# Mixture-of-experts rounds: token tiles held in TensorE and 512 weight columns moved past them, experts ranked by count, rounds of 192, 192, 128, 192, 128 and then 256 slots

## The chip, the cores and the metric

The kernel runs on one core of one Trainium2 chip. The metric is the device time of the program in microseconds (us). All matmuls of the part studied here are fp32-precision products put together from rounded halves, as described below.

## The reference

One inference step of a two-layer backbone on 640 tokens (128 of a prompt, 512 of a sample), width 1024. Each layer is a token mixer followed by a feed-forward part; in layer 0 that is a dense SwiGLU, in layer 1 it is a choice of 2 of 8 SwiGLU experts of inner width 1408. Only the last is touched by the change:

```python
logits = (hf @ router).astype(jnp.float32)
top_v, top_i = lax.top_k(logits, TOP_K)                       # TOP_K = 2, N_EXP = 8
wts = jax.nn.softmax(top_v, axis=-1)
gate = jnp.sum(jax.nn.one_hot(top_i, N_EXP, dtype=jnp.float32) * wts[..., None], axis=-2)
g, u = jnp.split(jnp.einsum('nd,edf->nef', hf, w_gu), 2, axis=-1)     # w_gu: 8 x 1024 x 2816
act = jax.nn.silu(g) * u * gate[..., None].astype(h.dtype)
return jnp.einsum('nef,efd->nd', act, w_down).reshape(B, T, D)        # w_down: 8 x 1408 x 1024
```

The 640 tokens make 1280 choices. Worked out from the reference and its inputs, experts 0 to 7 are chosen 177, 226, 132, 229, 147, 106, 48 and 215 times.

## The kernel before

The function `moe` runs `experts` (routing, then the expert rounds) and `combine` (gather of the two results of each token, residual, final norm). In `experts` the engines have one program each, tied together by semaphores.

Routing: the tokens are normed, the router product gives the logits, VectorE (DVE) works out each choice's slot (L2474 to L2482) and a table of rounds, ScalarE (ACT) copies the transposed tokens into `htok` (semaphore `h_tok`), and GpSimd (POOL) scatters them to `slots_h` in HBM by ten indirect DMAs (L2553). Slots are handed out in blocks of `BLK` = 256, as many blocks per expert as it needs, in the order of the experts.

Rounds: a hardware loop (`Fori`) does one block of 256 slots at a time. A round of the inputs used here belongs to one expert. In a round:

- SyncE (SP) loads the next block of slots and the expert's weights, 11 blocks j of 128 inner columns, each as two 512 KB gate-up transfers (L2246) and one 512 KB down transfer (L2248), into a ring `raw` of three slots.
- ACT rounds each piece to fp32r (`w_hi`, L2409) and DVE computes the rest (`w_lo` = raw - `w_hi`, L2514), so that a product is made of three: hi x hi, hi x lo, lo x hi.
- TensorE (PE) transposes the block of slots (L2335). For each j the gate-up product (L2360) holds 128x128 of weights as the stationary operand and moves 256 slots; its result lies with the inner columns on partitions, so it can be the stationary operand of the down product (L2347) as it is, which moves 512 weight columns. PE works on gate-up of j, then on down of j-1.
- ACT takes the silu of the gate half (L2421), DVE multiplies by the up half (L2524), and the two split the product into `act_hi` (L2425) and `act_lo` (L2526).
- At the end ACT and DVE split the next block (L2399, L2506), split the first weights of the next round, and copy the finished 256x1024 block out; POOL stores it (L2562).

## Time and profile before

| | |
|---|---|
| time, median of 3 runs | 2706.48 us (2704.94 to 2707.95) |
| profiled execution, first to last instruction | 2713.9 us |
| granted TensorE clock, mean over the span | 0.947 of full speed |
| PE busy | 2386.3 us, 88% |
| weight loads (PEld) busy | 2177.9 us, 80% |
| DVE busy | 1444.5 us, 53% |
| ACT busy | 1069.2 us, 39% |

No time of its own is given for the profiled execution beside its span, which is 7.4 us above the median of the runs. A busy engine in this table need not set the time; which one does is read stage by stage. The expert rounds run from 1893.42 us to about 2657.3 us of the span.

### The profile page before, as it was taken

What the parts mean: (1) busy time and instruction counts of PE and PEld (TensorE: products, weight loads), DVE (VectorE), ACT (ScalarE), POOL (GpSimd) and SP (SyncE); (2) the same over time, 40 slices, a digit from 0 to 9 for tenths busy, and PEclk for the clock granted to TensorE, in tenths of its full rate; (3) what the DMA queues carried; (4) which work ended last, traced back from release to release, by engine and by line L of the source; (5) the groups of instructions that cost most, each with busy time, mean ns of one, the idle gap of its engine ahead of it and who ended that gap; (6) DMA issues with size and microseconds to landing.
All of it is one profiled execution on the core that took longest, in us unless ns stands there. A gap on an engine that the chain in (4) does not pass through costs nothing. (4 is left out here: it accounts for less than half of the span.)

```text
span 2713.9 us, 47159 instructions
## 1 busy us (share of the span) xinstructions
PE 2386.3 (88%) x19349; PEld 2177.9 (80%) x19349; DVE 1444.5 (53%) x2038; ACT 1069.2 (39%) x1753; POOL 335.3 (12%) x347
## 2 busy tenths in 40 slices
PE   5996687888899999989967788895999999999993
PEld 4985465778899999989845667794999999999992
DVE  5577556774422222245665667743555555555556
ACT  4332136673422112143321366633444444444443
POOL 0055333001000000000553330012000000000002
PEclk8998899999899999989988999997999999999996
DMA  5332764703122322222127200025676676567664
GB/s 209 94 85 45 203 209 160 248 1 94 47 78 59 90 78 63 59 57 87 56 53 205 90 6 1 1 63 194 181 231 204 181 230 207 173 196 238 196 183 163
DMA packets 453116, 340.49 MB, mean 125 GB/s; under 512 B 90961, under 2 KB 421151, under 8 KB 451935
## 3 DMA queue, kind: packets, MB, share of 16 engines
q1 hardware_dynamic: 436383, 277.43, 35.2%
q10 hardware_dynamic: 11520, 41.95, 4.8%
...
## 5 line engine op out<-in xcount | busy, mean ns | idle before, releaser
L2360 PE MATMUL ps<-h_hi,w_hi 128*128 128x256 f32 x1408 | 399.5, 284 | 1.6 <-DVE h_lo L2506 1.6
L2360 PE MATMUL ps<-h_hi,w_lo 128*128 128x256 f32 x1408 | 399.0, 283 | 0.0
L2360 PE MATMUL ps<-h_lo,w_hi 128*128 128x256 f32 x1408 | 399.0, 283 | 0.0
L2514 DVE TENSOR_TENSOR w_lo<-w_raw,w_hi 128x2048 fp32r<-128x2048 f32 (+1 forms) x180 | 309.1, 1756 | 119.0 <-ACT w_hi L2409 119.0
L2360 PEld LDWEIGHTS ps<-h_hi,w_hi 128*128 128x128 f32 x1408 | 270.6, 192 | 4.7 <-issue 2.0
L2360 PEld LDWEIGHTS ps<-h_lo,w_hi 128*128 128x128 f32 x1408 | 270.7, 192 | 2.8
L2360 PEld LDWEIGHTS ps<-h_hi,w_lo 128*128 128x128 f32 x1408 | 270.6, 192 | 0.0
L2409 ACT CAST w_hi<-w_raw 128x2048 fp32r<-128x2048 f32 (+1 forms) x180 | 256.4, 1474 | 0.1
L2747 PE MATMUL ps<-ffn_h_hi,w_hi_ffn 128*128 128x320 f32 x704 | 161.9, 311 | 5.5 <-DVE ffn_h_lo L378 4.2
L2421 ACT ACTIVATE tokens_then_blocks<-ps 128x256 f32<-128x256 f32 x88 | 33.8, 384 | 325.8 <-PE ps L2360 325.7
L2747 PE MATMUL ps<-ffn_h_lo,w_hi_ffn 128*128 128x320 f32 x704 | 161.3, 311 | 0.0
L2747 PE MATMUL ps<-ffn_h_hi,w_lo_ffn 128*128 128x320 f32 x704 | 161.3, 311 | 0.0
L1849 DVE TENSOR_TENSOR p_lo<-ps,p_hi 128x512 fp32r<-128x512 f32 (+1 forms) x196 | 123.4, 631 | 50.9 <-ACT p_hi L1921 46.9
L2524 DVE TENSOR_TENSOR tokens_then_blocks<-tokens_then_blocks,ps 128x256 f32<-128x256 f32 x88 | 37.0, 421 | 199.0 <-ACT tokens_then_blocks L2421 199.0
L1921 ACT CAST p_hi<-ps 128x512 fp32r<-128x512 f32 (+1 forms) x196 | 106.3, 542 | 87.4 <-PE ps L1738 87.3
L1844 DVE TENSOR_REDUCE tm<-ps 128x1 f32<-128x768 f32 (+1 forms) x140 | 114.8, 821 | 43.6 <-PE ps L1714 29.0
L1738 PE MATMUL ps<-cst,tm 128*128 128x128 f32 x700 | 115.5, 284 | 23.1 <-DVE p_lo L1849 23.0
L571 PE MATMUL ps<-w_hi_in,h_hi 128*128 128x454 f32 x320 | 122.4, 382 | 4.6 <-DVE w_lo_in L152 3.1
L2747 PEld LDWEIGHTS ps<-ffn_h_hi,w_hi_ffn 128*128 128x128 f32 x704 | 118.3, 189 | 6.7 <-issue 6.7
L571 PE MATMUL ps<-w_lo_in,h_hi 128*128 128x454 f32 x320 | 119.2, 373 | 0.0
L2747 PEld LDWEIGHTS ps<-ffn_h_lo,w_hi_ffn 128*128 128x128 f32 x704 | 118.5, 189 | 0.0
L571 PE MATMUL ps<-w_hi_in,h_lo 128*128 128x454 f32 x320 | 118.5, 370 | 0.0
...
## 6 DMA issues: line engine op xcount, KB each, us to landing
...
```

What stands on the lines that cost most here:

```text
L571: mm = pe.matmul(ps[:, t, 0:TMT], x[:, 4 * half + k, t * P:(t + 1) * P], wt[:, tile % 2, k * TMT:(k + 1) * TMT], start=(half == 0 and k == ...
L1738: mm = pe.transpose(ring(j)[:, q * P:(q + 1) * P], prob_block(u, t, k) if t else prob_slot(u, 0), self.ident)
L1844: dve.tensor_reduce(low[:, u % 2, t:t + 1], score_tile(u, t), AX.X, ALU.min).then_inc(s["least"], 1)
L1849: dve.tensor_tensor(place(p_lo, j), turned(j), place(p_hi, j).bitcast(F32), ALU.subtract).then_inc(s["lo"], 1)
L1921: act.copy(place(p_hi, j), turned(j)).then_inc(s["hi"], 1)
L2360: mm = pe.matmul(ps[:, j % 2, half * BLK:(half + 1) * BLK], gu(wt, j, half, k), x[:, k, :], start=(k == 0 and n == 0), stop=(k == KC - 1 a ...
L2409: act.copy(whi[:, q, part], raw[:, q, part]).then_inc(s["hi_d" if down else "hi_u"], 1)
L2421: act.activation(sg[:, j % 2, :], ps[:, j % 2, 0:BLK], ACT.Silu).then_inc(s["silu"], 1)
L2514: dve.tensor_tensor(wlo[:, q, part], raw[:, q, part], whi[:, q, part].bitcast(F32), ALU.subtract).then_inc(s["lo_d" if down else "lo_u"], 1)
L2524: dve.tensor_tensor(g, g, ps[:, j % 2, BLK:2 * BLK], ALU.mult).then_inc(s["prod"], 1)
L2747: mm = pe.matmul(ps[:, 4 * (j % 2) + 2 * half + st, 0:b - a], wt[:, u, o:o + P], x[:, k, a:b], start=(k == 0 and m == 0), stop=(k == KC - ...
```

## The change

Experts are ranked by their number of choices, expert 0 put first in any case. The first five rounds are written out, with a fixed number of slots each (`SIZES`); the ranks that they serve are in `REGION`: 0, 3, 1, 4, 2. The three experts with the most choices get the 256-slot rounds of a loop, and what does not fit an expert's round goes to further rounds of 256. With the counts above that is the order 192 (177 choices), 192 (132), 128 (48), 192 (147), 128 (106), 256 (215), 256 (226), 256 (229), with no further round.

In a round the slots are tiles of 128 that are held as the stationary operand, and 512 weight columns (256 of gate, 256 of up) move: the 11 column blocks become `NU` = 6 units u, the last of half width, in 17 pieces of 1 MB (`ORDER`), which land in a ring of six slots (`RAW`) and are split into a ring of five (`HL`). The product now lies with the slots on partitions, so PE turns it (`turn_act`) before the down product, and ACT and DVE make `act_hi` and `act_lo` from the turned one. In a 192-slot round the tile of the last 64 slots ("few") is multiplied in plain fp32, from `raw`, without split: two matmuls of 64 stationary columns each, one writing partitions 0 to 63 and one 64 to 127.

Cut to its core:

```diff
-RMAX = 2 * T // BLK + NE - 1
+STATIC = 5
+RMAX = NE + 5
...
-        SL = 3
...
+        NU, PW, SMALL = 6, 2048, 64
+        ORDER = [("g", 0, 0), ("g", 0, 1), ("g", 1, 0), ("g", 1, 1), ("d", 0, 0)]
+        for u in range(2, NU):
+            ORDER += [("g", u, a) for a in range(2 if u < NU - 1 else 1)] + [("d", u - 1, 0)]
+        ORDER += [("d", NU - 1, 0)]
+        NP = len(ORDER)
+        RAW, HL = 6, 5
...
+            hT = raw[:, 2 * PW:2 * PW + KC * T].rearrange("p (c t) -> p c t", c=KC)
...
+            SIZES = (192, 192, 128, 192, 128)
+            REGION = (0, 3, 1, 4, 2)
...
+            def tiles_of(c):
+                return {128: (0,), 192: (1, 0), 256: (0, 1)}[c]
...
+            def groups(c):
+                return {128: ((0, 0, 3), (0, 1, 0)), 192: ((0, 0, 3), (1, None, 0), (0, 1, 1)),
+                        256: ((0, 0, 3), (0, 1, 0), (1, 0, 1), (1, 1, 3))}[c]
...
+            def wait_raw_free(eng, r, n):
+                if is_first(r) and n < 0:
+                    return
+                eng.wait_ge(s["w_hi"], count("pieces", r, n + 1))
+                eng.wait_ge(s["w_lo"], count("pieces", r, n + 1))
+                if isinstance(r, int) and size(r - 1 if n < 0 else r) == 192:
+                    kind, u, _ = ORDER[n % NP]
+                    if kind == "g":
+                        eng.wait_ge(s["gu"], tile_count(r - 1 if n < 0 else r, u, 1))
+                    else:
...
-                    for j in range(SL):
-                        load_w(0, j)
+                    for n in range(2):
+                        load_w(0, n)
+                    sp.wait_ge(s["h_tok"], 2 * NT)
+                    for n in range(2, RAW):
+                        load_w(0, n)
...
+                    def feed(r):
+                        sp.wait_ge(s["h_turned"], count("groups", r, 0, 1))
+                        load_block(next_size(r), region_of(r + 1) if isinstance(r, int) else r + (STATIC + 1))
...
+                    def multiply(r, u, tile):
+                        c = size(r)
+                        bank = gate_bank(c, u, tile)
+                        last = tile == tiles_of(c)[-1]
+                        if u == 0:
+                            pe.wait_ge(s["h_lo"], count("groups", r, 0, 1) if last else count("groups", r, 2))
+                        elif c > 128:
+                            pe.wait_ge(s["prod"], tile_count(r, u - 1, tile))
+                        elif u >= 2:
+                            pe.wait_ge(s["prod"], tile_count(r, u - 2, tile))
+                        if few(c, tile):
+                            half = columns(u) // 2
+                            for k in range(KC):
+                                n = at("g", u, k // 4 if u < NU - 1 else 0)
+                                if k in (0, 4):
+                                    pe.wait_ge(s[f"raw{raw_slot[n]}"], count_raw(raw_slot[n], r, landed[n]))
+                                w_ = gate_up_raw(u, k)
+                                for q in range(2):
+                                    mm = pe.matmul(ps[64 * q:64 * q + 64, bank, 0:2 * half].rearrange("p (h n) -> p h n", h=2),
+                                                   h_few[:, k], w_[:, :, q * half:(q + 1) * half], start=(k == 0), stop=(k == KC - 1))
+                            mm.then_inc(s["gu"], 1)
+                            return
+                        for k in range(KC):
+                            if k == 0 or k == 4 and u < NU - 1:
+                                pe.wait_ge(s["w_lo"], count("pieces", r, at("g", u, k // 4) + 1))
+                            for n, (x, wt) in enumerate(((hhi, whi), (hhi, wlo), (hlo, whi))):
+                                mm = pe.matmul(ps[:, bank, 0:2 * columns(u)], x[:, k, tile * P:(tile + 1) * P], gate_up(wt, u, k),
+                                               start=(k == 0 and n == 0), stop=(k == KC - 1 and n == 2))
...
+                        if few(c, tile) and u < NU - 1:
+                            mm = pe.transpose(ps[:, 2, 256:256 + P], act_tok[:, 1, 0:P], self.ident)
...
+                    def down(r, u, tile):
+                        c = size(r)
+                        pe.wait_ge(s["a_lo"], unit_done(r, u))
+                        pe.wait_ge(s["w_lo"], count("pieces", r, at("d", u) + 1))
+                        if u == 0 and not is_first(r):
+                            pe.wait_ge(s["y_act"], count("rounds", r))
+                            pe.wait_ge(s["y_dve"], count("rounds", r))
+                        for b in range(blocks_of(u)):
+                            st, sp_ = u == 0 and b == 0, u == NU - 1 and b == blocks_of(u) - 1
+                            if few(c, tile):
+                                for half in range(2):
+                                    mm = pe.matmul(ps[64 * half:64 * half + 64, 6, :], a_few[:, u % 2, b], down_rows_raw(u, b, half),
+                                                   start=st, stop=sp_)
...
+                    def work(r):
+                        c = size(r)
+                        order = tiles_of(c)
+                        coming = groups(next_size(r))
+                        for u in range(NU):
+                            for tile in order:
+                                multiply(r, u, tile)
+                            for tile in order[:-1]:
+                                turn_act(r, u, tile)
+                            if u:
+                                down(r, u - 1, 0)
+                                if c == 256:
+                                    down(r, u - 1, 1)
+                            turn_act(r, u, order[-1])
+                            if u == NU - 3:
+                                pe.wait_ge(s["blk_in"], count("blocks", r, PER["blocks"][next_size(r)], 1))
+                                turn_group(coming[0])
+                            if u == NU - 1:
+                                for n, g in enumerate(coming[1:]):
+                                    if n == 2:
+                                        pe.wait_ge(s["h_lo"], count("groups", r, 1, 1))
+                                    turn_group(g)
+                            if u and c == 192:
+                                down(r, u - 1, 1)
+                        for tile in range(len(order)):
+                            down(r, NU - 1, tile)
+                    for r in range(STATIC):
+                        work(r)
                     with pe.Fori(0, rounds) as r:
-                        pe.wait_ge(s["h_lo"], 4 * r + 4)
-                        for j in range(FC):
...
+                    def split(r, n, ahead=0):
+                        q = raw_slot[n]
+                        act.wait_ge(s[f"raw{q}"], count_raw(q, r, per_round[q] * ahead + landed[n]))
+                        wait_used(act, r, hl_before[n] + NP * ahead)
+                        act.copy(part(whi, n), raw_piece(n)).then_inc(s["w_hi"], 1)
...
+                    def work(r):
+                        c = size(r)
+                        order = tiles_of(c)
+                        coming = len(groups(next_size(r)))
+                        for u in range(NU - 1):
+                            gate(r, u, order[0])
+                            split(r, 3 * u + 2)
+                            for tile in order[1:]:
+                                gate(r, u, tile)
+                            take(r, u, order[0])
+                            split(r, 3 * u + 3)
+                            for tile in order[1:]:
+                                take(r, u, tile)
+                            split(r, 3 * u + 4)
+                        for tile in order:
+                            gate(r, NU - 1, tile)
+                        upper(r, next_size(r), 0, 1)
+                        for tile in order:
+                            take(r, NU - 1, tile)
+                        for m in range(1, coming):
+                            upper(r, next_size(r), m, 1)
+                        for n in range(2):
+                            split(r, n, 1)
+                        act.wait_ge(s["dn"], count("units", r, NU))
+                        if not is_first(r):
+                            act.wait_ge(s["y_free"], count("rounds", r))
+                        last = act.copy(y[:, 0, 0:512], ps[:, 4, :])
+                        if c == 192:
+                            last = act.copy(y[:, 0, 512:D], ps[:, 5, :])
+                        elif c == 256:
+                            last = act.copy(y[:, 1, 0:512], ps[:, 6, :])
+                        last.then_inc(s["y_act"], 1)
+                    for r in range(STATIC):
+                        work(r)
...
+                    chain(dve.scalar_tensor_tensor(out=key[:], in0=counts, scalar=16.0, in1=key0[:], op0=ALU.mult, op1=ALU.add))
+                    chain(dve.tensor_tensor(tri[:], bcast_mid(key[:], NE), bcast_last(key[:], NE), ALU.is_lt))
+                    chain(dve.tensor_reduce(region[:], tri[:], AX.X, ALU.add))
+                    chain(dve.tensor_scalar(wide[:], region[:], -1.5, None, ALU.add), wait=False)
+                    chain(dve.tensor_scalar(high[:], region[:], STATIC - 0.5, float(SMALL), ALU.is_ge, ALU.mult), wait=False)
+                    chain(dve.tensor_scalar(home[:], region[:], float(BLK), None, ALU.mult))
+                    chain(dve.tensor_tensor(wide[:], wide[:], wide[:], ALU.mult))
+                    chain(dve.tensor_scalar(wide[:], wide[:], 1.0, float(SMALL), ALU.is_ge, ALU.mult))
```

Of the routing, DVE's chain from the counts to the slots has 23 instructions where it had 8. The functions `gate`, `take`, `lower` and `split` of DVE stand in the same order as those of ACT in `work`.

Three places of the order of instructions. First PE, at the last column block of a 256-slot round before; `tokens_then_blocks` is the block of slots to be turned.

```order
L2360 MATMUL ps<-h_hi,w_hi 128x256
L2360 MATMUL ps<-h_lo,w_hi 128x256
L2360 MATMUL ps<-h_hi,w_lo 128x256
L2332 ISA
L2335 MATMUL ps<-cst,tokens_then_blocks 128x128 x4
L2347 MATMUL ps<-w_hi,act_hi 128x512 x2
L2347 MATMUL ps<-w_lo,act_hi 128x512 x2
L2347 MATMUL ps<-w_hi,act_lo 128x512 x2
```

The same engine with the change, in a unit of a 128-slot round; here `tokens_then_blocks` is the product to be turned.

```order
L2539 MATMUL ps<-w_lo,h_hi 128x512
L2539 MATMUL ps<-w_hi,h_lo 128x512
L2576 MATMUL ps<-w_hi,act_hi 128x512 x2
L2576 MATMUL ps<-w_lo,act_hi 128x512 x2
L2576 MATMUL ps<-w_hi,act_lo 128x512 x2
L2576 MATMUL ps<-w_hi,act_hi 128x512 x2
L2576 MATMUL ps<-w_lo,act_hi 128x512 x2
L2576 MATMUL ps<-w_hi,act_lo 128x512 x2
L2556 MATMUL ps<-cst,tokens_then_blocks 128x128 x2
L2539 MATMUL ps<-w_hi,h_hi 128x512
```

The gate-up product now moves 512 columns, and two transposes stand between the down product of unit u-1 and the gate-up product of unit u+1.

Second PE with the change in a 192-slot round, from the turn of the few tile to the next unit.

```order
L2549 MATMUL ps<-cst,tokens_then_blocks 128x128
L2576 MATMUL ps<-w_hi,act_hi 128x512 x2
L2576 MATMUL ps<-w_lo,act_hi 128x512 x2
L2576 MATMUL ps<-w_hi,act_lo 128x512 x2
L2556 MATMUL ps<-cst,tokens_then_blocks 128x128 x2
L2571 MATMUL ps<-w_raw,act_few 64x512 x4
L2531 MATMUL ps<-w_raw,tokens_then_blocks 64x256 x16
L2539 MATMUL ps<-w_hi,h_hi 128x512
```

The matmuls of 64 stationary columns stand beside those of 128, with a change between the two shapes four times in a unit.

Third DVE, before, in two column blocks of a round.

```order
L2524 TENSOR_TENSOR tokens_then_blocks<-tokens_then_blocks,ps 128x256
L2526 TENSOR_TENSOR act_lo<-tokens_then_blocks,act_hi 128x256
L2513 REGISTER_ALU
L2514 TENSOR_TENSOR w_lo<-w_raw,w_hi 128x2048
L2514 TENSOR_TENSOR w_lo<-w_raw,w_hi 128x1024
L2522 REGISTER_ALU
L2524 TENSOR_TENSOR tokens_then_blocks<-tokens_then_blocks,ps 128x256
```

And DVE with the change, in a unit of a 128-slot round and the start of the next; L2805 is the product with the up half, L2817 makes `act_lo`.

```order
L2805 TENSOR_TENSOR tokens_then_blocks<-tokens_then_blocks,ps 128x256
L2799 TENSOR_TENSOR w_lo<-w_raw,w_hi 128x2048
L2817 TENSOR_TENSOR act_lo<-ps,act_hi 128x2x128
L2799 TENSOR_TENSOR w_lo<-w_raw,w_hi 128x2048 x2
L2805 TENSOR_TENSOR tokens_then_blocks<-tokens_then_blocks,ps 128x256
```

A piece of weights now stands between the product and `act_lo`, and the second piece that the next unit needs stands behind `act_lo`, which waits for PE's transposes.

## Rows read from the trace of the kernel before

**Rows 1.** The head of the profile page.

```profile
span 2713.9 us, 47159 instructions
```

**Rows 2.** Busy time by stage, one round: us, busy of each engine, PEclk, DMA share, GB/s.

```profile
2083.00:2178.00 95.00, 95.00 (x677) 89.50 (x676) 50.61 (x50) 43.13 (x51) 0.75 (x1) 1.00 0.67 204
```

**Rows 3.** PE in order of time, last column blocks of a round: start us, us.

```profile
2079.01 0.60 PE L2335 MATMUL ps<-cst,tokens_then_blocks 128*128 128x128 f32 x4
2079.36 0.71 PE L2347 MATMUL ps<-w_hi,act_hi 128*128 128x512 f32 x2
2079.91 0.62 PE L2347 MATMUL ps<-w_lo,act_hi 128*128 128x512 f32 x2
2080.37 0.63 PE L2347 MATMUL ps<-w_hi,act_lo 128*128 128x512 f32 x2
...
2085.52 0.28 PE L2360 MATMUL ps<-h_lo,w_hi 128*128 128x256 f32 x1
2085.64 0.28 PE L2360 MATMUL ps<-h_hi,w_lo 128*128 128x256 f32 x1
```

**Rows 4.** PE in order of time, first and last matmuls of the rounds.

```profile
1893.42 0.57 PE L2360 MATMUL ps<-h_hi,w_hi 128*128 128x256 f32 x1 [1.59 <-DVE h_lo L2506]
...
2656.71 0.61 PE L2347 MATMUL ps<-w_hi,act_lo 128*128 128x512 f32 x2
```

**Rows 5.** Groups by line and shape, the round of rows 2: busy us, mean ns, idle before.

```profile
L2514 DVE TENSOR_TENSOR w_lo<-w_raw,w_hi 128x2048 fp32r<-128x2048 f32 x11 | 25.2, 2294 | 14.4 <-ACT w_hi L2409 14.4
L2409 ACT CAST w_hi<-w_raw 128x2048 fp32r<-128x2048 f32 x11 | 20.9, 1904 | 0.0
...
L2506 DVE TENSOR_TENSOR h_lo<-ps,h_hi 128x512 fp32r<-128x512 f32 x4 | 2.6, 685 | 0.6 <-ACT h_hi L2399 0.6
```

**Rows 6.** ACT and DVE in order of time, one column block.

```profile
2188.01 0.38 ACT L2421 ACTIVATE tokens_then_blocks<-ps 128x256 f32<-128x256 f32 x1
2188.88 0.41 ACT L2425 CAST act_hi<-tokens_then_blocks 128x256 fp32r<-128x256 f32 x1 [0.49 <-DVE tokens_then_blocks L2524]
2189.19 2.85 ACT L2409 CAST w_hi<-w_raw 128x2048 fp32r<-128x2048 f32 x2
...
2188.43 0.42 DVE L2524 TENSOR_TENSOR tokens_then_blocks<-tokens_then_blocks,ps 128x256 f32<-128x256 f32 x1 [2.30 <-ACT tokens_then_blocks L2421]
2191.12 3.43 DVE L2514 TENSOR_TENSOR w_lo<-w_raw,w_hi 128x2048 fp32r<-128x2048 f32 x2 [1.38 <-ACT w_hi L2409]
```

**Rows 7.** PE in the mixer: matmuls of 64 and 32 stationary columns, and the clock.

```profile
340.46 1.61 PE L1012 MATMUL ps<-conv_in_out 128*64 128x128 f32 x24
342.00 0.64 PE L1077 MATMUL ps<-G_decay,oA 128*32 128x256 f32 x8
342.57 0.27 PE L1143 MATMUL ps<-X_turned,Y 64*64 64x64 f32 x1
...
279.96 1.08 PE L1077 MATMUL ps<-G_decay,oA 128*32 128x256 f32 x8
280.82 1.08 PE L1077 MATMUL ps<-oA 128*32 128x256 f32 x8
...
340.50:343.00 2.50, 2.50 (x48) 1.82 (x48) 1.67 (x3) 0.90 (x2) 0.74 (x1) 1.00 0.84 323
279.96:281.80 1.84, 1.84 (x18) 0.59 (x16) 0.00 (x0) 0.48 (x1) 1.00 (x1) 0.50 0.67 111
```

**Rows 8.** Busy time by stage, a stretch of full DMA queues, columns as in rows 2.

```profile
2085.00:2099.00 14.00, 14.00 (x109) 13.55 (x108) 9.27 (x9) 8.31 (x10) 0.75 (x1) 1.00 1.08 355
```

**Rows 9.** The scatter of the tokens by stage, then DVE's chain ahead of it.

```profile
1863.00:1884.00 21.00, 1.55 (x8) 1.15 (x6) 8.43 (x13) 8.31 (x9) 13.73 (x10) 0.56 0.64 252
...
1861.51 0.22 DVE L2477 TENSOR_REDUCE first_slot<-by_expert 128x8 f32<-128x64 f32 x1
1861.76 0.20 DVE L2478 TENSOR_TENSOR place<-ps,first_slot 128x40 f32<-128x40 f32 x1
```

**Rows 10.** Busy time by stage, a stretch of the mixer with an interrupted PE.

```profile
1720.00:1760.00 40.00, 32.70 (x241) 30.74 (x240) 28.66 (x51) 26.49 (x61) 0.00 (x0) 0.91 0.01 1
```

536 lines of the change are left out of this document (338 added, 198 removed).

## The prediction

> **What bounds the kernel now.** I read the page's head first (span 2713.9 us [rows 1]), then busy time by stage. In a middle round PE is busy 95.00 of 95.00 us at the full clock, DVE 50.6, ACT 43.1, and the DMA engines 0.67 of the time at 204 GB/s [rows 2]: PE alone sets the length of a round. Next PE in order of time, for what an instruction really takes, since a busy time counts a matmul until its result is out. Starts lie 0.12 us apart for 256 moving columns, a pair of 512-column matmuls takes 0.46 us (0.229 each), four transposes 0.35 us (0.088 each) [rows 3]. A round has 528 gate-up matmuls, 132 down matmuls and 16 transposes: 528 x 0.12 + 132 x 0.229 + 16 x 0.088 = 63.4 + 30.2 + 1.4 = 95.0 us, which is the row. Eight rounds run from 1893.4 to 2657.3 us [rows 4], 763.9 us with a slow first microsecond or two. Eight is also what the counts give (none is over 256). So the rounds are 28% of the span, and of their 2048 slots 1280 hold a choice.
>
> **The change, part by part.**
>
> *Slots.* With the counts given, the rounds are 192, 192, 128, 192, 128, 256, 256, 256, no spill.
>
> *Full tiles.* A tile of 128 slots takes 120 gate-up matmuls of 512 columns and 24 of 256 (last unit): 120 x 0.229 + 24 x 0.12 = 30.4 us, and 66 down matmuls, 15.1 us [rows 3]. Turning the product is new: 11 transposes, 1.0 us. With 8 transposes for the block, 0.7 us, PE has 47 us of work in a 128-slot round and 94.1 in a 256-slot round, 0.9 less than now. The wider move pays 3.0 us there, since the 13 ns over the array's own time are paid once for 512 columns, not for 256; the turning takes 1.9 of them back.
>
> The Trainium skill ("TensorE: Matmul & The Clock Gate", Back-to-back issue gap) puts the gap at N/2.4 + 2.5 ns. By it wider moves would be worth 0.8 us, not 3.0, and a 256-slot round would come out 1 us longer than before. The rows show 13 to 16 ns, so I go by them.
>
> *The few tile.* Plain fp32 with 32 stationary columns in four groups: 8 records of 256 columns take 0.86 us at a granted clock of 0.50, the 1.2 GHz level, so four matmuls side by side, two records each, four clocks a column. With 64 stationary columns, two groups, 24 records of 128 columns take 1.54 us at the full clock, 0.064 each against 0.053 for the array alone: 11 ns more [rows 7]. So a few record costs 0.118 us at 256 columns and 0.224 at 512. Gate-up: 160 x 0.118 + 32 x 0.064 = 20.9 us; down: 44 x 0.224 = 9.9; in all 30.8 us where a full tile would take 45.5. The bounds: 28.2 at no overhead, and 34 at 20% over the array's time as in the 24 records. Changing the shape 24 times a round: the 8 records at full clock take 0.57 us, 0.06 more than their own time with a change ahead and behind [rows 7]; 0.05 each, 1.2 us. So 192 slots take 47 + 0.7 + 30.8 + 1.2 = 80 us.
>
> The skill ("TensorEngine Tiling (Array Packing)", Key Properties) says that a change of the tiling mode drains TensorE. A drain is some 0.16 us (a matmul's 0.28 us busy less its 0.12 us spacing [rows 3]), so by that rule it would be 4 us a round, 8 us more over three rounds. The 0.57 us speak against it.
>
> *Who waits in a 128-slot round.* Here PE's 8.4 us a unit come near what ACT and DVE need for three pieces, and the order of the instructions decides. From the end of a gate-up product: silu 0.15 us later, the ACT split of the next piece 0.31 after its start, the DVE split 1.93 after that start (2188.43, 2189.19, 2191.12) [rows 6], taking 2.29 us [rows 5]: first piece ready at 4.7 us, while PE has finished its down product (2.75) and turned (3.0). ACT and DVE make `act_hi` and `act_lo` before the second piece: `act_lo` until 5.1; `w_lo` of the second piece from 5.4 to 7.65. PE's first half of the gate-up product, 2.75 us, ends at 7.5, its second half starts at 7.75, and its result is there at 10.6. The unit takes 10.6 us, not 8.4. A round: 5.5 for the first product, four units of 10.6, 7.8 for the half-width one, 5.0 for the rest: 60.7 us, and 47 if I am wrong about the order. Weights are no bound: 18.3 MB in 60.7 us are 302 GB/s, against 355 with 512-byte to 4 KB packets mixed [rows 8], and loads have a lead of two units.
>
> *Between rounds* DVE splits the new block (0.69 us a group [rows 5]), then two pieces, 2.3 us each, before the first gate-up product can start. By the same steps the stall of PE is 2.2 us from 192 to 128 (the first piece's place is freed late, by the few tile's down product), 4.1 from 128 to 256, 2.6 from 256 to 256, none into a 192-slot round, whose few tile needs no split and covers the 2.3 us.
>
> *Routing.* DVE's chain has 15 instructions more ahead of the scatter, 0.25 us each [rows 9], some without a wait: 3.3 us. Four pieces (4.2 MB) are now loaded from the time that the tokens are turned, on the same DMA engines as the scatter, which moves 252 GB/s for 21 us [rows 9] of the 355 possible [rows 8]. The spare 2.2 MB in that time cover half, the rest is some 5 us of delay; a smaller first block gives 0.7 back. Taken: 7 us (3 if the loads slip in between, 12 if none does). Afterwards DVE copies the last block out behind a wider piece: 0.7 us.
>
> *The sum.* 3 x 80 + 2 x (60.7 + 2.2) + (94.1 x 3 + 4.1 + 2 x 2.6) + 1.5 for the slow first microseconds = 240 + 125.8 + 291.6 + 1.5 = 659 us for 763.9: 105 less. With 7.7 for routing and end it is 97 less. Against its own span that is 2713.9 - 97 = 2617; the runs' median lies 7.4 below the span, and I carry the difference over: 2706.5 - 97 = 2609 us.
>
> **The rivals.**
>
> *The order costs nothing* (PE keeps its pace because pieces are ready earlier than I follow): 27 us less in the 128-slot rounds, 9 to 14 at the round edges: 2570 us. For it: DVE has only 45 us of work in such a round. Against: both are in-order queues, and the second piece stands behind `act_lo`. 0.17.
>
> *More waits than I count*: the few tile at 34 us with a drain at each change (10 + 8 us), DMA hiccups in the 128-slot rounds, where each unit asks for 3.1 MB and a late piece stops ACT, DVE and PE in turn (10 to 20 us each). Or the clock: PE is busy 8.4 of 10.6 us a unit in a 128-slot round. In the mixer 32.7 of 40 us gave 0.91 [rows 10], which would add 5 us a round; if it stayed at the 1.2 GHz level, a unit would be 16.8 us and the two rounds 66 us longer. I put this case at 2665 us, 2632 to 2700. 0.26.
>
> *The few tile does not run side by side*, slower than before. With array time and drain one after the other, a 256-column record takes 0.213 + 0.16 us, a 512-column one 0.427 + 0.16: 160 x 0.373 + 32 x 0.267 + 44 x 0.587 = 94 us for 30.8, 190 us over three rounds: 2799 us. It takes half of that, 97 us, to lose the whole gain. Against it stand both rows at 0.057 to 0.064 us a record [rows 7]; for it that those products were short, and that here weights stream from `raw` while DMA writes there. 0.04.
>
> *The change doesn't do what it says*: other counts would bring spill rounds of 94 us each, and one takes all of the gain. Before, a count over 256 would have made a ninth round; there were eight, but 128 and 192 are not tested by that. 0.02, within 0.2% or slower.
>
> **How the numbers follow.** The forecast (2609 us, its own range 2585 to 2632) has 0.51. The two cases beside it hold 0.43; the range takes in the first down to 2568 and the lower half of the second: 2568 to 2655 leaves about 0.2 out. 0.2% is 5.4 us, about what a measurement of this kernel tells from no change. Faster: 0.94; same 0.01; slower 0.05.
>
> **What would show it.** In the profile after: PE starts 0.229 us apart at the gate-up line, 512 columns; records of 64 stationary columns 0.118 us apart; a 192-slot round of 80 us and a 256-slot round of 97 (94.1 if the edges cost nothing). In a 128-slot round PE waits twice a unit for `w_lo`, some 1.7 and 0.3 us, and the gate-up products end 10.6 us apart; 8.4 would be the first rival. The first gate-up product comes some 7 us later than 1893.4. I would be wrong if a wait for `raw` or the block's transfer stood in the 128-slot rounds, if PEclk fell there, or if the few tile took 40 us or more.

## The result and the profile after

The changed kernel takes 2635.4 us (median of 4 runs, 2629.4 to 2642.2), the kernel before 2707.2 us in the same comparison: a ratio of 0.9717, 95% interval 0.9689 to 0.9744. It is 72 us faster; 97 were forecast, 2609 us. The number lies inside the range, 26 us above the forecast and just outside the likeliest case's own range.

The head of the profile page after, which answers to [rows 1]: the span, PE's busy time and the granted clock in 40 slices.

```profile
span 2633.4 us, 42344 instructions
...
PE 2267.8 (86%) x17219; PEld 1955.9 (74%) x17219; DVE 1417.6 (54%) x1995; ACT 1029.8 (39%) x1666; POOL 334.8 (13%) x353
...
PEclk8999798999899999998997998989799999999996
```

The span is 80.5 us shorter. Busy time by stage comes next, cut at the first gate-up matmul of each of the eight rounds and at the end of the last down product (columns as in [rows 2], which they answer to).

```profile
1895.31:1978.37 83.06, 81.95 (x483) 57.30 (x485) 43.22 (x44) 36.08 (x37) 0.00 (x0) 0.98 0.57 183
1978.37:2061.19 82.82, 79.84 (x476) 55.98 (x473) 48.55 (x45) 39.58 (x40) 1.70 (x3) 1.00 0.70 235
2061.19:2126.78 65.59, 54.90 (x237) 43.12 (x237) 41.89 (x32) 33.33 (x33) 1.66 (x3) 0.92 0.88 295
2126.78:2209.63 82.85, 79.86 (x475) 56.03 (x475) 48.79 (x46) 40.09 (x40) 0.56 (x1) 1.00 0.66 218
2209.63:2277.24 67.61, 53.41 (x238) 42.31 (x238) 44.77 (x35) 37.68 (x37) 1.64 (x3) 0.95 0.90 311
2277.24:2377.94 100.70, 97.04 (x459) 80.30 (x459) 49.87 (x47) 40.15 (x46) 0.56 (x1) 0.98 0.62 202
2377.94:2477.05 99.11, 95.46 (x458) 79.11 (x458) 50.47 (x48) 40.91 (x48) 0.73 (x1) 1.00 0.60 196
2477.05:2573.98 96.93, 95.44 (x458) 79.12 (x458) 48.30 (x47) 38.79 (x46) 0.71 (x1) 1.00 0.58 189
```

The expert stage takes 678.7 us, where it took 763.9 [rows 4]; 659 had been forecast. So the direction and most of the size are in the rounds, as worked out, and 20 us of the miss are too. Where PE was busy without a break before [rows 2], it is not any more: 11 to 14 us of each 128-slot round are idle, and the granted clock is below 1.00 in them and in two others.

PE in order of time at the start of the first 128-slot round shows both (start us, us, and in brackets the idle time before and what ended it).

```profile
2061.19 0.47 PE L2539 MATMUL ps<-w_hi,h_hi 128*128 128x512 f32 x1 [1.88 <-DVE w_lo L2799]
2061.50 0.40 PE L2539 MATMUL ps<-w_lo,h_hi 128*128 128x512 f32 x1
...
2063.03 0.63 PE L2539 MATMUL ps<-w_hi,h_hi 128*128 128x512 f32 x1
2063.45 0.63 PE L2539 MATMUL ps<-w_lo,h_hi 128*128 128x512 f32 x1
...
2069.46 0.44 PE L2556 MATMUL ps<-cst,tokens_then_blocks 128*128 128x128 f32 x2 [0.93 <-DVE tokens_then_blocks L2805]
2073.12 0.80 PE L2539 MATMUL ps<-w_hi,h_hi 128*128 128x512 f32 x1 [3.22 <-DVE w_lo L2799]
...
2075.42 0.63 PE L2539 MATMUL ps<-w_hi,h_lo 128*128 128x512 f32 x1
2075.84 0.63 PE L2539 MATMUL ps<-w_hi,h_hi 128*128 128x512 f32 x1
...
2086.43 0.47 PE L2539 MATMUL ps<-w_hi,h_hi 128*128 128x512 f32 x1 [1.74 <-DVE w_lo L2799]
2086.73 0.40 PE L2539 MATMUL ps<-w_lo,h_hi 128*128 128x512 f32 x1
2086.96 0.40 PE L2539 MATMUL ps<-w_hi,h_lo 128*128 128x512 f32 x1
```

Four idle stretches in 26 us. After the one of 1.88 us and the one of 3.22 us matmuls of 512 columns start 0.42 us apart, not 0.229: TensorE is at the 1.2 GHz level. The second unit's gate-up product lasts from 2073.12 to 2081.73, 8.6 us for 24 matmuls, where the same product in a later unit takes 5.84 to 5.95.

DVE in order of time in the second and third unit of that round, to be read against the steps forecast from [rows 6]:

```profile
2082.19 0.42 DVE L2805 TENSOR_TENSOR tokens_then_blocks<-tokens_then_blocks,ps 128x256 f32<-128x256 f32 x1 [4.39 <-ACT tokens_then_blocks L2645]
2083.99 2.29 DVE L2799 TENSOR_TENSOR w_lo<-w_raw,w_hi 128x2048 fp32r<-128x2048 f32 x1 [1.37 <-ACT w_hi L2639]
2086.20 0.42 DVE L2817 TENSOR_TENSOR act_lo<-ps,act_hi 128x256 fp32r<-128x256 f32 x1
2086.93 4.49 DVE L2799 TENSOR_TENSOR w_lo<-w_raw,w_hi 128x2048 fp32r<-128x2048 f32 x2 [0.31 <-ACT w_hi L2639]
2092.76 0.42 DVE L2805 TENSOR_TENSOR tokens_then_blocks<-tokens_then_blocks,ps 128x256 f32<-128x256 f32 x1 [1.34 <-ACT tokens_then_blocks L2645]
```

Gate to gate is 10.57 us, as forecast. DVE stands idle for 3.0 us of it (1.37, 0.31 and 1.34), each time for ACT, and the piece that PE wants is done only at 2086.28, just ahead of PE's start at 2086.43. Ahead of the rounds, PE's last wait for the scatter and the first gate-up product:

```profile
1886.84 4.61 PE L2499 MATMUL ps<-w_hi 128*128 128x512 f32 x10 [25.14 <-DMA slots_h<-tokens_then_blocks,slot_of_choice]
...
1895.31 1.12 PE L2531 MATMUL ps<-w_raw,tokens_then_blocks 128*64 128x256 f32 x4 [0.78 <-DVE tokens_then_blocks L2791]
```

The routing stage's first matmul starts at 1836.43 (1839.48 in the kernel before), so from there to the first gate-up product it is 58.9 us for 53.9 before. To the first issue of the scatter it is 26.0 us for 23.6, from there until PE is released 24.4 for 19.9, and from that to the first product 8.5 for 10.5.

### The profile page after: what moved, and what is told of

It is laid out like the page before. It is cut to its first block and busy times, and to the rows that moved or that the text cites. A ratio compares the mean times of both kernels' runs of the same rounds, so it can differ in the third digit from the quotient of the medians.

```text
span 2633.4 us, 42344 instructions
## 1 busy us (share of the span) xinstructions
PE 2267.8 (86%) x17219; PEld 1955.9 (74%) x17219; DVE 1417.6 (54%) x1995; ACT 1029.8 (39%) x1666; POOL 334.8 (13%) x353
## 5 line engine op out<-in xcount | busy, mean ns | idle before, releaser
L2539 PE MATMUL ps<-w_hi,h_hi 128*128 128x512 f32 (+1 forms) x528 | 205.9, 390 | 32.2 <-DVE w_lo L2799 32.2
L2539 PE MATMUL ps<-w_lo,h_hi 128*128 128x512 f32 (+1 forms) x528 | 200.1, 379 | 0.0
L2539 PE MATMUL ps<-w_hi,h_lo 128*128 128x512 f32 (+1 forms) x528 | 199.8, 378 | 0.0
L2539 PEld LDWEIGHTS ps<-w_hi,h_hi 128*128 128x128 f32 x528 | 101.5, 192 | 63.3 <-issue 26.5
L2645 ACT ACTIVATE tokens_then_blocks<-ps 128x256 f32<-128x256 f32 (+2 forms) x84 | 29.0, 346 | 277.5 <-PE ps L2539 232.9
L3079 PEld LDWEIGHTS ps<-ffn_h_hi,w_lo_ffn 128*128 128x128 f32 x704 | 118.6, 189 | 0.0
L2143 DVE SCALAR_TENSOR_TENSOR xT<-ps,mod,xT 128x128 f32<-128x128 f32 (+2 forms) x96 | 36.3, 433 | 152.9 <-PE ps L3090 102.7
L1912 ACT ACTIVATE tm<-ps,tm 128x768 f32<-128x768 f32 (+1 forms) x140 | 111.7, 798 | 14.7 <-DVE tm L1845 14.6
## 6 DMA issues: line engine op xcount, KB each, us to landing
slots_h<-tm SPq DMA_DIRECT2D x14, 1024.0 KB, 11.2
```

The costliest lines, as they stand in the source:

```text
L1912: act.activation(prob_slot(u, t), x.rearrange("p (a n) -> p a n", a=3) if t else x, ACT.Exp, scale=-1.0, bias=low[:, u % 2, t:t + 1], accu ...
L2143: dve.scalar_tensor_tensor(out=x, in0=self.ps[:, 2 * (m % 4) + half, a - a0:b - a0], scalar=self.mod[:, l, gate, m, j:j + 1], in1=x, op0=A ...
L2539: mm = pe.matmul(ps[:, bank, 0:2 * columns(u)], x[:, k, tile * P:(tile + 1) * P], gate_up(wt, u, k), start=(k == 0 and n == 0), stop=(k == ...
L2645: act.activation(act_tok[:, tile, 0:wd], ps[:, gate_bank(c, u, tile), 0:wd], ACT.Silu).then_inc(s["silu"], 1)
L3079: mm = pe.matmul(ps[:, 4 * (j % 2) + 2 * half + st, 0:b - a], wt[:, u, o:o + P], x[:, k, a:b], start=(k == 0 and m == 0), stop=(k == KC - ...
```

## The experiments

All round lengths below are taken as above, from the first gate-up matmul of a round to that of the next; "stage" is from the first of them to the end of the last down product. A ratio is to the kernel before on the same chip. Microseconds:

```
kernel       rounds 1 to 7                                      stage
changed      83.06 82.82 65.59 82.85 67.61 100.70 99.11         678.7
again        83.08 82.83 65.56 82.83 67.64 100.67 99.09         678.7
all256       99.38 100.73 99.12 99.13 100.63 100.59 99.09       797.2
nofew        99.15 99.73 67.50 99.72 67.52 100.64 99.15         732.0
oneside      111.44 110.34 64.36 110.38 67.71 100.42 100.78     762.4
first128     83.13 82.83 62.99 82.83 66.61 100.72 99.14         675.2
both128      81.60 82.86 51.37 82.85 55.56 100.69 99.11         651.0
fill128      83.08 82.83 62.73 82.82 64.73 101.81 99.14         674.1
both_late    80.25 81.46 51.85 81.49 55.82 101.02 102.62        654.9
loadslate    82.60 82.83 65.32 82.85 67.49 100.64 99.13         679.4
edge         83.35 82.82 64.08 82.85 66.71 98.20 98.57          673.9
combo        80.23 81.47 51.89 81.49 54.92 99.77 98.55          645.7
combo_fill   81.08 81.47 51.62 81.48 54.67 98.14 98.58          644.2
```

**all256**: every round 256 slots wide.

```
-            SIZES = (192, 192, 128, 192, 128)
+            SIZES = (256, 256, 256, 256, 256)
...
-                    for g in groups(size(0)):
+                    for n, g in enumerate(groups(size(0))):
+                        if n == 3:
+                            pe.wait_ge(s["h_lo"], 1)
                         turn_group(g)
...
-                    chain(dve.tensor_tensor(wide[:], wide[:], high[:], ALU.add))
+                    chain(dve.tensor_scalar(wide[:], wide[:], 0.0, float(P), ALU.mult, ALU.add))
```

The wait is for the fourth group of the first block, and the last pair gives every expert a wide slot region.

> All eight expert rounds are made 256 slots wide; tokens stay the stationary operand and 512 weight columns move, the order of the work is the changed kernel's. So this is the first part of the change alone (and the routing chain, less what sorts experts by size). Theory (the gain comes from the round sizes, the new orientation by itself costs a little): a 256-round of the changed kernel took 99.1 us from start to start and the last one 97, so the expert stage is 7 x 99.1 + 97 = 791 us against 678.7 in the changed kernel, and the time 2635 + 112 = 2747 us, about 1.5% slower than the kernel before, whose eight rounds took 763.9 us. Rival (the orientation itself brings a part of the gain, as fewer and longer matmuls): a round is no longer than the 95.5 us of the kernel before, stage 764 us or less, time 2720 us or less.

Ratio 1.0140 (1.0111 to 1.0169): the new orientation, with its order of work, loads and routing chain but without the sizes, makes the kernel 1.4% slower; all of the gain comes from the sizes. The stage is 6 us longer than expected, which is the clock: four drops of 1.6 us. Busy time by stage, the first 11 us of the second, third and fourth round (the column after the five engines' busy times is the granted clock):

```profile
2001.30:2012.30 11.00, 11.00 (x41) 8.92 (x42) 5.12 (x5) 2.90 (x4) 0.77 (x1) 0.84 0.81 284
2102.03:2113.03 11.00, 11.00 (x49) 9.07 (x50) 6.21 (x5) 3.18 (x5) 0.75 (x1) 1.00 0.81 284
2201.15:2212.15 11.00, 11.00 (x49) 9.06 (x50) 5.99 (x5) 2.91 (x4) 0.70 (x1) 1.00 0.82 278
```

All three follow the same 2.24 us of waiting for `w_lo`; in one the clock fell to 0.84 over these 11 us and the round was 1.6 us longer. That happened in four of the seven rounds behind such an edge.

**nofew**: the 192-slot rounds become 256-slot ones.

```
-            SIZES = (192, 192, 128, 192, 128)
+            SIZES = (256, 256, 128, 256, 128)
...
-                    chain(dve.tensor_scalar(wide[:], wide[:], 1.0, float(SMALL), ALU.is_ge, ALU.mult))
-                    chain(dve.tensor_tensor(wide[:], wide[:], high[:], ALU.add))
+                    chain(dve.tensor_scalar(wide[:], wide[:], 1.0, float(P), ALU.is_ge, ALU.mult))
```

The wait of all256 for the first block's fourth group is in it too; the last lines fit the slot regions to the sizes.

> The three rounds of 192 slots become rounds of 256: the 64-token tile with fp32 matmuls in two column groups goes, its place is taken by a second full tile in three split passes. Two rounds of 128 stay. Theory (the two column groups run side by side, a 192-round is worth 82.9 us against 99.1): three rounds x 16.2 us = 48.6 us longer, 2684 us. Rival (the small tile saves less, since its shape changes and its first unit's 1.11 us wait for its turned activations go with it): 256-rounds in these places take 96 us, three x 13 = 39 us, 2674 us. If the small tile brought nothing, 2635 us.

Ratio 0.9906 (0.9876 to 0.9935), 2691 us on a chip where the kernel before took 2716.6: 53 us more than the changed kernel by the stage, 48.6 expected. The few tile is worth 16 to 17 us a round; the rest of the difference is 1.9 us in one 128-slot round and a clock drop of 1.6 us in the last round.

**oneside**: the pairs of the few tile on the same 64 partitions.

```
-  mm = pe.matmul(ps[64 * q:64 * q + 64, bank, 0:2 * half] ...
+  mm = pe.matmul(ps[0:64, bank, 0:2 * half] ...
-  mm = pe.matmul(ps[64 * half:64 * half + 64, 6, :], a_few ...
+  mm = pe.matmul(ps[0:64, 6, :], a_few ...
```

The flags that start and end a sum go with it (not shown).

> The two matmuls of each pair of the few tile (64 stationary tokens) write the same 64 partitions instead of partitions 0 to 63 and 64 to 127, so they cannot lie side by side; same count, same columns, same data. The outputs of the 64-token tiles are not those of the reference. Theory (the pair runs side by side in the changed kernel: 0.11 us a record of 256 columns, where one alone would need twice that): 0.21 to 0.24 us a record, the unit's few gate-up 7 us instead of 3.6 and few down 3.8 instead of 1.9, some 5.3 us a unit, 32 us a round, 95 us for the three: 2730 us, and the gain over the kernel before is gone. Rival (the matmuls are back to back anyway and the pairing brings nothing): 2635 us.

2723.6 us in its one run, the kernel before 2714.3 (median). The groups by line and shape over the two first rounds (busy us, mean ns) have the same 320 and 88 records; first the changed kernel:

```profile
L2531 PE MATMUL ps<-w_raw,tokens_then_blocks 128*64 128x256 f32 x320 | 37.9, 391 | 0.8 <-DVE tokens_then_blocks L2791 0.8
...
L2571 PE MATMUL ps<-w_raw,act_few 128*64 128x512 f32 x88 | 21.5, 606 | 0.0
```

and then oneside:

```profile
L2531 PE MATMUL ps<-w_raw,tokens_then_blocks 128*64 128x256 f32 x320 | 72.3, 385 | 0.8 <-DVE tokens_then_blocks L2791 0.8
L2571 PE MATMUL ps<-w_raw,act_few 128*64 128x512 f32 x88 | 40.3, 599 | 0.0
```

Each record is busy as long as before, but the time that they cover is 1.9 times as long: in the changed kernel two of them are under way at once. Without it a 192-slot round takes 110.4 us, more than a 256-slot one, and the whole gain is gone, as the rival in the prediction said it would be.

**first128** and **both128**: the order of the splits in the 128-slot rounds, on ScalarE and VectorE alike. first128 has the first condition of this diff alone, both128 the two.

```
+                            if c == 128:
+                                split(r, 3 * u + 2)
                             gate(r, u, order[0])
-                            split(r, 3 * u + 2)
+                            if c != 128:
+                                split(r, 3 * u + 2)
...
+                            if c == 128:
+                                split(r, 3 * u + 3)
                             take(r, u, order[0])
-                            split(r, 3 * u + 3)
+                            if c != 128:
+                                split(r, 3 * u + 3)
```

> In the rounds of 128 slots alone, ScalarE and VectorE split the first weight piece of the next unit ahead of the unit's gate and not behind it. Theory (the piece waits only because of the order: VectorE cannot start on it before the silu and gate of the unit, which come after all of the unit's matmuls): the waits of TensorE for w_lo go, 1.74 us in each of four or five units and 3.22 us in the first, and the clock stays up in the second unit (8.6 us for its gate-up products becomes 5.5). Unit 8.7 to 9.0 us instead of 10.6, some 14 us for each of two rounds, 2607 us (2603 to 2615). Rival 1 (VectorE is the bound of these rounds at three splits of 2.29 us with gate and act_lo, and the wait only moves to the second piece): unit 10.2 us or more, 2630 us or more. Rival 2 (the transfers bind: three pieces of 1.05 MB in 8.7 us are 362 GB/s, about what was seen at best): waits for the raw pieces take the place, unit 9.5 us or more, 2620 us.

Ratio 0.9703 (0.9679 to 0.9727), which can't be told from 0.9717. PE and then DVE in order of time in first128, one unit:

```profile
2092.63 0.50 PE L2539 MATMUL ps<-w_hi,h_hi 128*128 128x512 f32 x1 [1.85 <-DVE w_lo L2807]
...
2088.47 0.42 DVE L2825 TENSOR_TENSOR act_lo<-ps,act_hi 128x256 fp32r<-128x256 f32 x1 [2.84 <-ACT act_hi L2654]
2090.28 6.70 DVE L2807 TENSOR_TENSOR w_lo<-w_raw,w_hi 128x2048 fp32r<-128x2048 f32 x3 [1.38 <-ACT w_hi L2639]
```

PE's wait now stands between the two halves of the product; the next ones are at 2103.28 and 2113.87, so the unit is 10.65 us as before. The stage is 3.4 us shorter, mostly by the clock: the second unit's gate-up product takes 7.3 and 7.6 us in the two rounds, its wait not counted, for 8.6. I had expected a gain of some 28 us and got none that the median shows: the first rival was right that the wait moves, but not in its reason. VectorE is not full; it waits 2.84 us for `act_hi`, and the piece that PE wants is queued behind that.

> As first128, and the second piece too is split ahead of the turned activations (act_hi, act_lo), in the 128-slot rounds alone. In first128 the 1.74 us wait ahead of a unit's gate-up products became a 1.85 us wait between their two halves and the unit stayed at 10.65 us. Theory (two in-order queues with one piece too many behind the round trip; both edits are needed together): no wait for w_lo inside a unit, unit 8.7 to 9.0 us, which is TensorE's own work, 1.8 us x 5 less for each round and some 4 us in the first unit as before, about 24 us less than the changed kernel, ratio to before 0.963. Rival 1 (VectorE's own work of 7.6 us a unit and its round trips bind at 9.5 to 10 us): 10 us less, 0.968. Rival 2 (transfers: 3.15 MB in 8.8 us are 358 GB/s, 372 was the most seen in a stretch of the changed kernel): waits for the raw pieces appear, unit 9.2 us or more.

Ratio 0.9617 (0.9595 to 0.9640). The two 128-slot rounds by stage, without the edge behind the second:

```profile
2064.62:2115.99 51.37, 49.66 (x238) 39.54 (x238) 41.62 (x32) 34.12 (x33) 1.66 (x3) 1.00 1.07 364
2198.84:2250.90 52.06, 50.67 (x237) 41.29 (x237) 42.10 (x33) 34.95 (x35) 1.63 (x3) 0.97 1.07 366
```

Inside the units only one wait of PE for `w_lo` is left, 0.45 us in the second product of each round; a unit takes 8.4 to 9.2 us, 8.7 on average, and the stage is 27.7 us shorter. The DMA engines are at 1.07 of their time with 364 GB/s over a whole round, and the second rival is half right: ACT now waits for raw pieces, eight times in the first of the two rounds (7.2 us) and four times in the second (3.5 us), where in the changed kernel it never does in these rounds. The longest of them:

```profile
2102.64 1.91 ACT L2639 CAST w_hi<-w_raw 128x2048 fp32r<-128x2048 f32 x1 [1.64 <-DMA w_raw<-in_moe_w_gu]
```

Little of it reaches PE: the shortest units are at the 8.4 us that its own work takes, the longest 0.8 us above. The transfers are the next bound here.

**fill128**: matmuls that no one reads, in the first unit of the 128-slot rounds.

```
+                            if u == 0 and c == 128:
+                                for _ in range(3):
+                                    pe.matmul(ps[:, 7, :], hhi[:, 0, 0:P], gate_up(whi, 0, 0), start=True, stop=True)
                             turn_act(r, u, order[-1])
+                            if u == 0 and c == 128:
+                                for _ in range(10):
+                                    pe.matmul(ps[:, 7, :], hhi[:, 0, 0:P], gate_up(whi, 0, 0), start=True, stop=True)
```

> In the first unit of each 128-slot round TensorE gets 3 matmuls ahead of the turning of the activations and 10 behind it, which multiply pieces that it has already, into a bank that no one reads; about 2.9 us at 0.229 us each, in 4.15 us that it stands idle today. Nothing else moves. Theory (the second unit's gate-up products take 8.6 us and not 5.5 because the granted clock fell to the lower level after the idle time): granted clock near 1.0 in those stretches, these products 5.5 to 6 us, 2.5 to 3 us less for each of two rounds, 2629 to 2630 us. Rival (the products are slow because they wait within the unit for w_lo, the clock is only a sign of it): no change in the 8.6 us beyond 0.5, 2635 us.

Ratio 0.9691 (0.9666 to 0.9717). The second unit's gate-up product by stage, first in the changed kernel:

```profile
2073.12:2081.73 8.61, 8.61 (x25) 6.83 (x26) 4.68 (x3) 1.49 (x1) 0.00 (x0) 0.64 1.07 369
```

and in fill128:

```profile
2069.14:2074.86 5.72, 5.72 (x25) 4.77 (x26) 4.68 (x3) 1.49 (x1) 0.00 (x0) 1.00 1.07 378
```

It starts 11.92 us behind the round's first product as before (11.93), so PE's work starts no sooner, and takes 5.72 us for 8.61; the idle time left ahead of it is 0.90 us for 3.22. Both rounds are 2.9 us shorter. That is not chance between executions: the same product took 7.1 to 8.6 us in all twelve 128-slot rounds of the six profiled kernels that have this 3.22 us wait, and 5.72 us in both rounds of fill128. The clock is the cause, and idle time ahead of it is what lowers it. The round behind the second of them is 1.1 us longer, because the clock drop behind its 3.51 us edge lasts longer (13.9 us for the first 48 matmuls, not 12.8), so the stage gains 4.6 us. The ratios' intervals overlap; the proof is in these rows, not in the medians.

**both_late**: as both128, and in the first unit of the wider rounds the last turning stands behind the next product.

```
                             for tile in order:
                                 multiply(r, u, tile)
+                                if u == 1 and c > 128 and tile == order[0]:
+                                    turn_act(r, 0, order[-1])
...
-                            turn_act(r, u, order[-1])
+                            if u or c == 128:
+                                turn_act(r, u, order[-1])
```

> As both128, and in the 192- and 256-slot rounds the first unit's last turning of activations comes behind the next unit's first gate-up product, so that TensorE has work while ScalarE and VectorE gate the product (in the changed kernel it stands idle there for 1.11 to 1.14 us in each of these six rounds, and 0.35 us more in the 256-slot ones). Theory (the first unit of a round lacks the down product that covers these steps in the other units): these waits go, 3 x 1.11 + 3 x 1.5 = 7.8 us less than both128. Rival (the piece behind the late turning, and the down product that needs it, are late instead): the gain is 3 us or less, with a wait for w_lo at the first down product.

Ratio 0.9639 (0.9613 to 0.9665), no gain over both128. The 192-slot rounds are 1.4 us shorter each, the 256-slot ones 0.3, 3.5 and 3.5 us longer. PE in order of time in the second unit of a 256-slot round, the 5 us behind it by stage, and DVE in that unit:

```profile
2368.94 0.50 PE L2539 MATMUL ps<-w_hi,h_hi 128*128 128x512 f32 x1 [1.92 <-DVE w_lo L2811]
...
2369.00:2374.00 5.00, 5.00 (x16) 3.96 (x17) 0.00 (x0) 0.20 (x1) 0.00 (x0) 0.66 0.70 210
...
2364.84 0.42 DVE L2829 TENSOR_TENSOR act_lo<-ps,act_hi 128x256 fp32r<-128x256 f32 x1
2366.59 2.29 DVE L2811 TENSOR_TENSOR w_lo<-w_raw,w_hi 128x2048 fp32r<-128x2048 f32 x1 [1.33 <-ACT w_hi L2643]
```

The theory holds for the 192-slot rounds, the rival for the others: the turned activations are late, the piece split behind them is late, and PE waits for it (1.92 us for the 1.5 saved, 0.4 net). The rest of the 3.5 us is the clock, twice 1.6 us: at the round's edge, and behind this very wait, where it is granted at 0.66.

**loadslate**: pieces 2 to 5 of the first expert behind the scatter.

```
-                    for n in range(2, RAW):
-                        load_w(0, n)
                     sp.wait_ge(s["table"], 1)
...
                     load_block(size(0), region_of(0))
+                    for n in range(2, RAW):
+                        load_w(0, n)
```

> The loads of pieces 2 to 5 of the first expert (4.2 MB) are issued after the scatter has landed and after the first block, not while it runs. Theory (they take the DMA engines from the scatter: first scatter to last landing is 24.3 us with them and was 19.8 us in the kernel before): 20 us again, the first gate-up product 4 us earlier in its distance from the routing stage's start, 4.5 us less in all. Rival (the scatter's time is set by its own issue on the Pool queue, 4.5 us is from somewhere else): 24 us as before, and the pieces come late: piece 2 is wanted 14 us after the first product, 4.2 MB take 11 to 12 us at 372 GB/s, no loss or up to 3 us slower.

Ratio 0.9695 (0.9671 to 0.9719), which can't be told from 0.9717. The first issue of the scatter, then PE in order of time ahead of the rounds:

```profile
1867.23 1.22 POOL L2874 DMA_INDIRECT slots_h<-tokens_then_blocks,slot_of_choice  x1 [16.62 <-ACT tokens_then_blocks L2629]
...
1886.02 4.09 PE L2499 MATMUL ps<-w_hi 128*128 128x512 f32 x10 [19.54 <-DMA slots_h<-tokens_then_blocks,slot_of_choice]
...
1894.12 1.12 PE L2531 MATMUL ps<-w_raw,tokens_then_blocks 128*64 128x256 f32 x4 [0.36 <-DVE tokens_then_blocks L2791]
```

The routing stage starts at 1841.32 here, so it is 52.8 us to the first product, 6.1 less than in the changed kernel and 1.1 less than in the kernel before. From the first issue of the scatter at 1867.23 until its last landing lets PE go at 1886.02 it is 18.8 us for 24.4. The other profiles bear this out: 24.4 to 25.0 us in all ten with the early loads, 18.8 in all three without (this one, combo and combo_fill). The rounds are as long as before, so the later pieces are in time.

**again**, **edge**, **combo** and **combo_fill** shared a chip.

> The changed kernel unaltered, as the measure for the three beside it on this chip. Every theory expects the ratio to before seen already, 0.972, and the same waits in the expert rounds. What it adds is a second profiled execution: if the time ahead of the routing stage (1836.4 us in the changed kernel's profile, 1839.5 in that of the kernel before) differs by some us again, that part of the difference between the two spans belongs to no change.

Ratio 0.9703 (0.9677 to 0.9729), the same stage to 0.1 us. The routing stage starts at 1842.12 us: 5.7 later than in the first profile, by nothing in the program.

The edit of edge, alike in `upper` and `lower`:

```
-                        for m in range(1, coming):
+                        for m in range(1, min(coming, 2 if next_size(r) == 256 else 4)):
                             lower(r, next_size(r), m, 1)
                         for n in range(2):
                             split(r, n, 1)
+                        for m in range(2, coming if next_size(r) == 256 else 2):
+                            lower(r, next_size(r), m, 1)
```

> Only the order at the end of a round that leads into a 256-slot one: ScalarE and VectorE split the next expert's first two weight pieces behind the second of the block's four groups, not behind the fourth. Theory (the wait at the edge is VectorE's queue: four groups of 0.69 us, then two pieces of 2.29): it becomes 1.4 us shorter each time, 3.5 to 2.1 us once and 2.16 to 0.8 us twice, 4.2 us in all, ratio 0.970. Rival (the place of the second piece is freed late, by the last down product, and sets the wait): the wait stays within 0.3 us, 0.972.

Ratio 0.9705 (0.9685 to 0.9726), equal to again. PE at the start of a 256-slot round in edge, and ACT and DVE ahead of it:

```profile
2373.77 0.50 PE L2539 MATMUL ps<-w_hi,h_hi 128*128 128x512 f32 x1 [1.18 <-DVE w_lo L2801]
...
2372.63 1.91 ACT L2639 CAST w_hi<-w_raw 128x2048 fp32r<-128x2048 f32 x1 [1.23 <-PE ps L2576]
...
2374.56 2.29 DVE L2801 TENSOR_TENSOR w_lo<-w_raw,w_hi 128x2048 fp32r<-128x2048 f32 x1 [0.85 <-ACT w_hi L2639]
```

The wait fell by 1.0 us, not 1.4, and half of that came back between the two halves of the product: an undisturbed round is 98.57 us for 99.1. The second piece can't be split before the last down product has freed its place (the release by `PE ps L2576`). Both theories are half right, and 1.6 us in three rounds is too little to see in the median. The other 3.2 us by which this stage is shorter are the clock: the drop behind the first unit costs 1.5 us less in each 128-slot round and the one behind the first 256-slot edge is missing, while the first product of the second 128-slot round got one of 1.6 us that it didn't have before.

combo is both128, the late turning for `c == 192` alone, loadslate and edge.

> Four edits together: the split order of both128, the late turning in the first unit of the 192-slot rounds alone (in both_late these rounds lost their wait and the 256-slot ones got one of 1.92 us), the loads behind the scatter, and the edge order. Theory (the parts lie in different places and add up): both128 at 0.9617, less 3 x 1.4 us, less 6 us, less 4.2 us, 14.4 us or 0.0053: ratio 0.956, some 43 us less than the changed kernel. Rival (the stalls are one pool, shortening one lengthens another): 0.960 or more.

Ratio 0.9564 (0.9543 to 0.9584): 2597.4 us for 2716.4, 40.5 less than again. The parts add up, 43 having been expected. Its expert stage by busy time:

```profile
1893.76:2539.46 645.70, 629.46 (x3278) 489.06 (x3278) 375.61 (x337) 306.84 (x320) 7.55 (x13) 0.99 0.71 238
```

combo_fill adds these, four more ahead of the first unit's last turning (not in the 192-slot rounds) and six behind the last down product of the fifth round:

```
+                        for _ in range({128: 7, 192: 0, 256: 3}[c]):
+                            pe.matmul(ps[:, 2, :], whi[:, 4, 0:P], whi[:, 4, 0:512], start=True, stop=True)
```

> Combo, with matmuls that no one reads where TensorE stands idle at round edges and in first units: 7 at the start of a 128-slot round, 3 at the start of a 256-slot one and 6 more ahead of the first of these, 4 ahead of the first unit's last turning. Theory (an idle stretch of 1.9 us or more is followed by 5 to 6 us at the lower clock in some of the rounds, which costs 1.6 us each): 3 to 5 us less than combo, ratio 0.9545 to 0.955. Rival (the fill is itself in the way where the wait is shorter than it, or the idle stretches of combo are short enough already): equal to combo within 2 us.

Ratio 0.9554 (0.9529 to 0.9580), which can't be told from combo; the stage is 1.5 us shorter. The rival holds: in combo one clock drop of 1.6 us is left to be had in the 256-slot rounds, and filling got that one. The drops behind the edges of the two 128-slot rounds are gone too, but these rounds are only 0.3 us shorter each, and the first round, which is not filled, came out 0.9 us longer.

## Why the prediction came out as it did

The direction, the places and most of the size came out as worked out; the forecast is 26 us low, and no single term makes the miss. The stage by its terms, in us; measured values are the round lengths less the wait for `w_lo` at the edge behind them:

```
term                              forecast   measured
three rounds of 192, slow start    241.5      245.0   (83.06, 80.94, 80.97)
two rounds of 128                  121.4      129.7   (65.59, 64.09)
three rounds of 256                282.3      292.4   (98.54, 96.94, 96.93)
edges                               13.7       11.6   (1.88, 1.88, 3.52, 2.16, 2.17)
sum                                658.9      678.7
```

*The 192-slot rounds.* Right. The few tile was sized from rows of another stage [rows 7], and runs side by side as they said: the 160 wide gate-up records take 18.1 us a round (3.6 for 32 of them) where I had 18.9. The 3.5 us too many are a wait of 1.11 us for `act_few` in each first unit, which I didn't have. Without it a round is 79.8, under the 80 forecast with 1.2 us for all changes of shape. Those changes I had counted wrongly: the trace has 16 a round (18 in the first), two in a middle unit and not four as I wrote ahead of the prediction too (the few tile's down product and its next gate-up product stand side by side). Each costs about 0.10 us: from the last few record of a gate-up product to the next full one it is 0.309 us in all 15 cases, where the next few one would start after 0.209, and from a full down matmul to a few one 0.327 us, where full ones start 0.229 apart. That is 1.6 us a round, so 24 times 0.05 was near the sum by two errors against each other. The Trainium skill ("TensorEngine Tiling (Array Packing)", Key Properties) says that changing the tiling mode drains TensorE; the trace agrees that a change costs something, 0.10 us, less than the 0.16 us that I had estimated for a drain.

*The 128-slot rounds.* The order of the queues, the step with most steps in it, was right: unit 10.6 us forecast, 10.54 to 10.65 measured in the later units, and both128 shows that it is the order, since 8.7 us follow when two pieces move ahead of the round trips. My detail was off, though without effect: PE waits once a unit, 1.74 us, not twice. What failed is that the clock was taken as staying at the full level: I had worked out 5 us a round for a lower one from [rows 10], but put it into a rival and left it out of the sum, and my own sign of being wrong, PEclk falling in these rounds, came true. It cost 7.4 of the 8.3 us, 2.9 in each second unit (fill128) and 1.6 in the first product of one round.

*The 256-slot rounds* are the term that was mis-sized, 94.1 forecast and 97 measured. (My own prices add up to 94.3: twice 46.4 for a full tile and 1.4 for the block.) In the first unit there is no down product to cover gate and turning, and PE waits 1.14 us for `act_lo` and 0.36 for `w_lo`, 1.5 in each of three rounds. I had followed a middle unit and a round's edge, and not the unit between. Another 1.6 us is the clock behind the 3.52 us edge. The remaining 4 us, 1.3 a round, are small and spread: a round without its two waits has 95.4 us of PE. The spacing of 0.229 us held; so did the turning. But the 0.9 us that a wide round was to have less than the 95.0 of before did not come. The gap by the formula of the Trainium skill ("TensorE: Matmul & The Clock Gate", Back-to-back issue gap) is not what the rows show, 0.216 us against 0.229 for 512 columns. That its forecast for the round, 1 us longer than before, was nearer than mine is chance, since the round is longer mostly by the two waits and not by the gap. all256 shows the outcome whole: 1.4% slower.

*The edges* were forecast at 2.2, 4.1 and 2.6 us and measured 1.88, 3.52 and 2.16, none into a 192-slot round: right.

*Routing and end.* 7 us forecast from the routing stage's start to the first product, 4.9 measured. The chain ahead of the scatter costs 2.4 us (forecast 3.3) and the scatter beside the loads 4.5 (forecast 5). Behind the scatter it is 2.1 us less and not 0.7: the block is smaller, and the few tile, which now comes first, needs no split; all256, whose first block is wide, takes 9.3 us there and not 8.5. loadslate shows that the early loads cost 6.1 us, more than the whole of the 4.9. The end behind the last down product went from 56.6 to 59.4 us, 2.8 where I had 0.7; in again it is 57.4, so two of these us come and go with the execution.

*The carrying over.* The stage, routing and end give 19.7 - 2.1 + 2.1 = 19.7 of the 26 us between forecast and result. Of the 80.5 us between the spans three were already there when the routing stage began (1839.48 to 1836.43), which brings the miss down to 16.7; that start was seen from 1833.0 to 1843.4 in kernels that are the same up to it. The other 9.4 us come of my last step: I took 97 us off a median that lay 7.4 below the span of the profiled execution, and with the change the median lies 2.0 above it. The runs of before in this comparison are 2704.9 to 2715.0 us, and the medians on the other chips 2714.3 to 2716.6, so 7.4 us is within what executions of it differ by. Where the profiled execution of before lost them isn't settled.

*The rivals.* "The order costs nothing" is out: 10.6 us a unit. "The few tile does not run side by side" is out, and oneside shows what it would have cost: 83.7 us on the stage, less than the 190 I gave it, and still more than the gain. Of the 190, 113 were drains; the 77 that are left for the array's own time are near what was measured. Of "more waits than I count" the clock came true at 9 us in all and the waits at 8, without drains of the size that it took and without a late transfer; so the result lies between that case and the forecast. "The change doesn't do what it says" is out as well: there are eight rounds of the forecast sizes.
